# Sixteen residual tiles, and the queries and keys of 32 heads, turned by VectorE from swapped blocks instead of by TensorE

## The chip, the cores and the metric

The kernel runs on one core of one Trainium2 chip, as one program in one launch. The metric is its device time in microseconds (us). The core has a matrix engine (TensorE, PE in the profile), a vector engine (VectorE, DVE), a scalar engine (ScalarE, ACT), a general one (GpSimd, POOL), and the engine that issues the weights' DMAs (SyncE, SP).

## The reference

Two blocks of a model run on the same 256 tokens of width 2048, in float32. The first (`first_block`) is one layer: norm, a projection to the queries, keys and values of 8 + 8 heads and to two gates, two kinds of attention over heads of 128, gated output projections, a feed-forward part of width 5632, and a gated side input. The second (`second_block`) has an even layer (short convolutions, a chunked state space part, attention to 256 memory tokens) and an odd layer (latent attention with 16 heads, and memory attention again). Cut to what the change touches:

```python
# first block: per head of 128
z = q @ k.T * scale                      # causal: stick breaking (sb), or with bias, softmax (ca)
log_keep = where(past, log_sigmoid(-z), 0.0)
between = cumsum(log_keep, reverse=True) - log_keep
a = where(past, exp(log_sigmoid(z) + between), 0.0);  y = a @ v
# residual sums, each of them then normed and multiplied by the next weights
x = x + merged @ w_mix_out
x = x + (silu(g_ff) * u_ff) @ w_ffn_out
x = x + sigmoid(h @ w_ple_gate) * (p @ w_ple_in)
x = x + concatenate([y_a, y_b, y_m]) @ w_out0
# odd layer, latent attention, 16 heads: 128 columns without and 64 with rotation
q_full = concatenate([q_nope, q_rope]);  k_full = concatenate([k_nope, k_rope])
y_c = causal_block_attention(q_full, k_full, v) * silu(z_c)
```

## The kernel before

**The stream.** All weights lie in one stream of 919 units of 512 KB, each 2 chunks of 128 rows by 512 columns. SP loads them one after the other into a ring of four slots, `raw`. For each unit ACT makes the high part `w_hi` (rounded; line 1241), DVE the low part `w_lo` = raw - high (line 1756), and PE runs `unit`: eight matmuls with the high part (line 730: two chunks, two halves of the tokens, high and low part of the activations) and four with the low part (line 736). ACT and DVE work three units ahead (`LEAD`), in a ring of four, so a slot is free when PE has ended the unit before.

**The order.** Everything else is placed beside the stream by hand. A stage is a loop over blocks of 512 output columns and over units; before the split of unit u + 3 (on ACT and DVE) and before unit u (on PE) a hook is called with the unit's number, and what it issues stands there in the engine's queue. All engines run in order. POOL's queue carries the stores and loads of activations. The stages in the trace's order: mem, win (20 blocks of 8 units; the last eight carry the heads), out, mix, ffn, ffo, ple, gate, then ein, dt, ez, sc, eout of the even layer and olow, omem, uq, ukv, zc, oout of the odd one.

**The heads of win.** `attend` handles four heads per iteration of 16 units, four iterations. Head j begins at unit 3j: PE transposes its two halves of q and k (line 808), ACT copies them out of PSUM (`qk_t`, line 1350), PE makes the scores one unit later (lines 815, 816), DVE adds the mask (`z_sb`, line 1867), ACT and DVE make the probabilities, PE transposes them at 3j + 5, DVE copies them (`p_t`, line 1900), and PE makes y at 3j + 6 (line 828). ACT and DVE split y into `y_t_hi` and `y_t_lo` (line 1904). POOL loads q, k and v of a head with two DMAs.

**The residual tiles.** A stage that ends in a sum of the residual stream gives four tiles of 256 x 512. DVE adds (line 1959), POOL stores the tile, and in the following block, at `TURN_AT` = 3, PE transposes it by `turn_tile` (line 767, eight transposes), with ACT and DVE taking the high and low parts straight from PSUM. Already in the kernel before, the eleven `h` tiles of the ffn go another way: POOL stores the tile to `d_h`, loads it back with four DMAs that swap blocks of 32 rows (`h_b`, line 550), and DVE turns within blocks of 32 x 32 (line 1996).

**The latent heads.** `latent_heads` of zc starts a head every second unit: four transposes for q and k (line 1169), and for each second head two for the rotated part (line 1174); a copy by ACT (line 1694), scores one unit later (lines 1184, 1185). DVE also makes the block's gated tile (line 2462) and the heads' output rows (line 2436). Heads of the attention to memory are done by `mem_job`, whose step 0 transposes loaded queries and keys (`m_qkv`, line 916).

## Time and profile before

| | us |
|---|---|
| median of 3 runs (2696.89 to 2697.67) | 2696.9 |
| profiled execution | 2698.77 |
| its span | 2697.2 |
| PE busy | 2679.3 (99%) |
| DVE busy | 1522.2 (56%) |
| ACT busy | 1364.0 (51%) |
| POOL busy | 239.9 (9%) |
| DMA | 597.00 MB, 221 GB/s in the mean |

The profile is one execution; the time of a kernel is the median of runs, so a difference worked out in the trace is taken from the profiled execution and then set against the median. PE is busy nearly all of the span, so what counts in every view is what PE does and what it waits for; the idle time of the others is no cost. L12 stands for line 12 of the kernel, PEld for the loads of weights into PE, which run beside its matmuls.

### The profile page before, as it was taken

How to read it: one execution, taken by the hardware profiler on the slowest of the kernel's cores; microseconds unless marked ns; L12 is line 12 of the kernel's file. 1: busy time of each engine (PE TensorE's matmuls, PEld its weight loads, DVE VectorE, ACT ScalarE, POOL GpSimd, SP SyncE). 2: the span in 40 equal slices, each digit the busy share in tenths (PEclk: the TensorE clock that was granted, in tenths of full speed). 3: DMA queues.
4: the chain of work that ended last, by engine and by line, in shares of the span. 5: the costliest groups of instructions: out<-in, count | busy, mean ns of one | idle time of the engine just before them, and what ended most of it. 6: DMA issues, size and time to landing. Idle time of an engine off the chain costs nothing.

```text
span 2697.2 us, 36246 instructions
## 1 busy us (share of the span) xinstructions
PE 2679.3 (99%) x12375; PEld 2229.3 (83%) x12375; DVE 1522.2 (56%) x1771; ACT 1364.0 (51%) x1822; POOL 239.9 (9%) x344
## 2 busy tenths in 40 slices
PE   9999999999999999999999999999999999999998
PEld 7888888888888888888888888888888889788887
DVE  6444455656555555555454664446777755446754
ACT  6544455654444444444444554446575445555543
POOL 2100011100000000000000001001110000121200
PEclk9999999999999999999999999999999999999999
DMA  8976666666766667676666767667666766675565
GB/s 304 307 227 216 215 230 213 196 233 218 226 208 209 226 208 222 210 225 224 205 207 205 245 216 223 207 209 246 219 223 219 252 207 211 221 267 197 177 215 163
DMA packets 165441, 597.00 MB, mean 221 GB/s; under 512 B 20080, under 2 KB 20128, under 8 KB 164576
## 3 DMA queue, kind: packets, MB, share of 16 engines
q1 hardware_dynamic: 133632, 485.03, 54.9%
q0 software_dynamic: 30992, 109.53, 12.5%
q8 instruction: 66, 1.08, 0.2%
q10 hardware_dynamic: 720, 1.11, 0.1%
q14 instruction: 31, 0.25, 0.0%
HBM read 547.83 MB, written 49.33 MB: 221 GB/s over the span
## 4 chain that ended last, share of the span: by engine, by line
PE 95%; DVE 2%; ACT 1%; issue 1%; DMA 1%; POOL 0%; POOLq 0%; ACTq 0%; SPq 0%; DVEq 0%
PE acc L730 59%; PE acc L736 30%; PE turn L767 1%; DVE w_lo L1756 1%; PE turn L1032 1%; ACT w_hi L1241 0%; PE ps_s L1184 0%; PE ps_s L1185 0%; PE ps_y L828 0%; DMA m_qkv<-d_mem 0%; PE ps_y L937 0%; PE turn L1169 0%; PE ps_s L922 0%; PE ps_s L816 0%; PE turn L1191 0%
## 5 line engine op out<-in xcount | busy, mean ns | idle before, releaser
L1756 DVE TENSOR_TENSOR w_lo<-raw,w_hi 128x1024 fp32r<-128x1024 f32 x919 | 1120.4, 1224 | 940.5 <-ACT w_hi L1241 933.3
L1241 ACT ACTIVATE w_hi<-raw 128x1024 fp32r<-128x1024 f32 x919 | 966.6, 1059 | 926.9 <-PE acc L736 888.9
L730 PE MATMUL acc<-w_hi,x_t_hi 128*128 128x512 f32 (+1 forms) x2400 | 951.5, 396 | 0.0
L730 PE MATMUL acc<-w_hi,x_t_lo 128*128 128x512 f32 (+1 forms) x2400 | 933.0, 389 | 0.0
L736 PE MATMUL acc<-w_lo,x_t_hi 128*128 128x512 f32 (+1 forms) x2400 | 639.9, 388 | 0.0
L736 PEld LDWEIGHTS acc<-w_lo,x_t_hi 128*128 128x128 f32 x2400 | 450.5, 188 | 92.3
L730 PEld LDWEIGHTS acc<-w_hi,x_t_hi 128*128 128x128 f32 x2400 | 450.9, 188 | 90.3 <-issue 1.9
L730 PEld LDWEIGHTS acc<-w_hi,x_t_lo 128*128 128x128 f32 x2400 | 450.9, 188 | 90.1 <-issue 1.9
L730 PE MATMUL acc<-w_hi,ff_t_hi 128*128 128x512 f32 x352 | 137.2, 390 | 0.0
L730 PE MATMUL acc<-w_hi,ff_t_lo 128*128 128x512 f32 x352 | 137.0, 389 | 0.0
L736 PE MATMUL acc<-w_lo,ff_t_hi 128*128 128x512 f32 x352 | 94.1, 389 | 0.0
L730 PE MATMUL acc<-w_hi,z_t_hi 128*128 128x512 f32 x224 | 87.8, 392 | 0.0
L730 PE MATMUL acc<-w_hi,z_t_lo 128*128 128x512 f32 x224 | 87.2, 389 | 0.0
L736 PEld LDWEIGHTS acc<-w_lo,ff_t_hi 128*128 128x128 f32 x352 | 66.1, 188 | 13.8
L730 PEld LDWEIGHTS acc<-w_hi,ff_t_hi 128*128 128x128 f32 x352 | 66.1, 188 | 13.6
L730 PEld LDWEIGHTS acc<-w_hi,ff_t_lo 128*128 128x128 f32 x352 | 66.1, 188 | 13.6
L406 POOL DMA_DIRECT2D d_x<-tile x16 | 11.7, 730 | 559.0 <-DVE tile L1959 352.0
L736 PE MATMUL acc<-w_lo,z_t_hi 128*128 128x512 f32 x224 | 59.9, 389 | 0.0
L730 PE MATMUL acc<-w_hi,o_t_hi 128*128 128x512 f32 x144 | 56.5, 392 | 0.0
L730 PE MATMUL acc<-w_hi,o_t_lo 128*128 128x512 f32 x144 | 56.1, 389 | 0.0
L730 PE MATMUL acc<-w_hi,lat_t_hi 128*128 128x512 f32 x136 | 56.0, 412 | 0.0
L730 PE MATMUL acc<-w_hi,lat_t_lo 128*128 128x512 f32 x136 | 54.0, 397 | 0.0
(394 smaller groups left out, 2601.5 us busy)
## 6 DMA issues: line engine op xcount, KB each, us to landing
raw<-stream SPq DMA_DIRECT2D x919, 512.0 KB, 4.2
d_in<-tile POOLq DMA_DIRECT2D x20, 512.0 KB, 3.7
d_ev<-tile POOLq DMA_DIRECT2D x20, 512.0 KB, 4.4
d_x<-tile POOLq DMA_DIRECT2D x16, 512.0 KB, 4.0
xin<-d_x POOLq DMA_DIRECT2D x16, 512.0 KB, 7.3
qkv<-d_in POOLq DMA_DIRECT2D x32, 192.0 KB, 3.7
d_h<-tile POOLq DMA_DIRECT2D x11, 512.0 KB, 5.9
h_b<-d_h POOLq DMA_DIRECT2D x44, 128.0 KB, 4.2
```

Source lines behind the costliest of these rows:

```text
L406: pool.dma_start(dst[:, :, bass.ds(b.times(NBW), NBW)], tile[slot][:, :, :])\
L730: nc.tensor.matmul(out, src[x][:, chunk + c, t * P:(t + 1) * P], w_hi[:, s, w], start=first and c == 0 and x == 0, stop=False)
L736: mm = nc.tensor.matmul(acc[2 * bank + t][:, 0:width], src[0][:, chunk + c, t * P:(t + 1) * P], w_lo[:, s, w], start=False, stop=last and ...
L767: mm = nc.tensor.transpose(turn[h][:, (c * TH + t) * P:(c * TH + t + 1) * P], src[:, t, at:at + P], ident[:, :])
L1032: nc.tensor.matmul(turn[t][:, w], dec[:, t, h * P:(h + 1) * P], xdt[:, t, w], start=True, stop=True)
L1241: nc.scalar.activation(w_hi[:, u.slot, :], raw[:, u.slot, :], ACT.Copy).then_inc(hi_ready, 1)
L1756: nc.vector.tensor_tensor(w_lo[:, s, :], raw[:, s, :], w_hi[:, s, :].bitcast(F32), ALU.subtract).then_inc(lo_ready, 1)
```

## The change

Three kinds of transposes leave PE, and a step is moved.

Residual tiles: 16 of 20 (`BY_DVE`; out 3 of 4, mix 3, ffo 4, gate 3, eout 3) are written with their columns regrouped, so that each run of 128 stored columns holds one 32-column piece of each of the four 128-column chunks; the later readers read them back through the same view. After the store has landed, POOL loads four blocks (32 partitions x 8 x 128, 128 KB each) into `r_b` (in the out stage through `d_h` into `h_b`), DVE turns them (`turn_blocks`, 128 x 1024) and ACT and DVE make the high and low parts from SBUF. `RES_AT` and `X4_AT` give the units of these steps, the fourth tile of ffo is turned in the gate stage, and out takes units 6 and 7.

Heads of win: the columns of the weights are permuted on the host, q and k of a head are loaded by four DMAs of 32 partitions x 8 x 64 (64 KB) and v by a fifth, and DVE turns q and k two units before the scores (`HEAD_AT_UNIT`: heads at 1, 3, 6, 9). Only the first head's later steps thereby come one unit later than before.

Latent heads: two heads are a pair. Eight block DMAs, one of the rotated part and two of v are loaded per pair, into one buffer for q and one for k, which POOL refills when DVE has turned the pair before; DVE turns a pair with two instructions (`turn_pair`) at every fourth unit. The transposes of the rotated part stay on PE.

The second layer's memory heads (`mem_job(1, ...)`) run one unit later, their last step in the first unit of zc.

```diff
+BY_DVE = {"out": 3, "mix": 3, "ffo": 4, "gate": 3, "eout": 3}
+RES_AT = {"mix": (5, 6, 7), "ffo": (5, 6, 7), "gate": (6, 7, 7)}
+X4_AT = {(2, 1): 0, (2, 6): 1, (3, 5): 2}
+HEAD_AT_UNIT = (1, 3, 6, 9)
+    def natural(a):
+        return a.rearrange("p (c b i) -> p c b i", c=4, i=SQ)
+    def regrouped(a, on=True):
+        return a.rearrange("p (b c i) -> p c b i", b=4, i=SQ) if on else natural(a)
...
         def load_head(j, J, m):
-            for t in range(TH):
-                src = heads[j % 2][:, t, :, bass.ds(m, 1), :].rearrange("p m h d -> p m (h d)")
-                pool.dma_start(qkv[j][:, t, :, :], src).then_inc(at_loaded[j], 16)
+            for b in range(HD // SQ):
+                src = d_in[:, bass.ds(m.times(2 * HD, 3072 * (j % 2) + 2 * SQ * b), 2 * SQ)]
+                pool.dma_start(qk_b[j][b * SQ:(b + 1) * SQ, :, :], src.rearrange("(a j) n -> j a n", j=SQ))\
+                    .then_inc(at_loaded[j], 16)
+            src = d_in[:, bass.ds(m.times(HD, 3072 * (j % 2) + 2048), HD)]
+            pool.dma_start(v_h[j][:, :, :], halves(src)).then_inc(at_loaded[j], 16)
...
+        def load_blocks(dst, src, n):
+            pool.wait_ge(turned, 2 * n)
+            for b in range(P // SQ):
+                pool.dma_start(dst[b * SQ:(b + 1) * SQ, :, :],
+                               src[:, b * P:(b + 1) * P].rearrange("(a j) n -> j a n", j=SQ)).then_inc(blocks_in, 16)
...
-                store_tile(new, At(b), b % 2, s_, v_)
+                store_tile(halves(new), At(b), b % 2, s_, v_)
                 if b < 2:
-                    load_tile(old, At(b + 2), b % 2, [])
+                    load_tile(halves(old), At(b + 2), b % 2, [])
+                if b < BY_DVE[stage]:
+                    pool.wait_ge(tile_moved[b % 2], 16 * (STORED[stage] + b // 2 + 2))
+                    load_blocks(r_b, new[:, b * NBW:(b + 1) * NBW], TURN[turns] + b)
...
-            load_latent(J)
+        for j in range(1, 8):
+            pool.wait_ge(l_qk, j)
+            if j + 1 < 8:
+                load_rope(j + 1)
+            load_q(j)
+            load_k(j)
+            for J in (2 * j, 2 * j + 1):
+                load_v(J)
...
-                if p == 3 * j:
-                    pe.wait_ge(at_loaded[j], At(0, i, 1).times(32, 32))
-                    pe.wait_ge(at_qk, J.times(1, 1))
-                    for x in range(2):
-                        for t in range(TH):
-                            mm = nc.tensor.transpose(turn[0][:, (2 * x + t) * P:(2 * x + t + 1) * P],
-                                                     qkv[j][:, t, x, :], ident[:, :])
-                if p == 3 * j + 1:
+                if p == HEAD_AT_UNIT[j] + 1:
...
-                        if b:
-                            turn_tile(At(turns + b - 1), tile[(b - 1) % 2], *ready(b - 1))
...
-                    mem_job(1, At(4 + j), p - 7 * j - 5)
+                    mem_job(1, At(4 + j), p - 7 * j - 6)
...
-                    nc.scalar.activation(qk_t[s][:, :], turn[0][:, :], ACT.Copy).then_inc(at_qk, 1)
-                    nc.scalar.activation(lqk[s][:, :], turn[0][:, :], ACT.Copy).then_inc(l_qk, 1)
...
+        def turn_blocks(n, count, src, dst):
+            dve.wait_ge(blocks_in, count)
+            dve.wait_ge(turn_lo, 2 * n + 2)
+            nc.vector.transpose(dst[:, :].rearrange("p (c a i) -> p c a i", c=4, i=SQ),
+                                src[:, :, :].rearrange("p a (c i) -> p c a i", c=4)).then_inc(turned, 2)
...
+                if p == HEAD_AT_UNIT[j] - 1:
+                    dve.wait_ge(at_loaded[j], At(0, i, 1).times(80, 80))
+                    dve.wait_ge(at_scores, J.times(1, 1))
+                    nc.vector.transpose(qk_t[s][:, :].rearrange("p (x a i) -> p x a i", x=2, i=SQ),
+                                        qk_b[j][:, :, :].rearrange("p a (x i) -> p x a i", x=2))\
+                        .then_inc(at_qk, 1)
...
-                    last = nc.vector.tensor_tensor(tile[b % 2][:, t, :], acc[2 * (b % 2) + t][:, :],
-                                                   xin[b % 2][:, t, :], ALU.add)
+                    last = nc.vector.tensor_tensor(regrouped(tile[b % 2][:, t, :], b < BY_DVE[stage]),
+                                                   natural(acc[2 * (b % 2) + t][:, :]),
+                                                   regrouped(xin[b % 2][:, t, :], stage == "ffo" and b < BY_DVE["mix"]),
+                                                   ALU.add)
...
+        def turn_pair(j):
+            dve.wait_ge(at_loaded[0], AT_LOADS + 128 * (j + 1))
+            for x, src in enumerate((q_b, k_b)):
+                last = nc.vector.transpose(lqk[:, :, x, :].rearrange("p s (a i) -> p s a i", i=SQ),
+                                           src[:, :, :].rearrange("p a (s i) -> p s a i", s=2))
+            last.then_inc(l_qk, 1)
...
+            if p % 4 == 0 and 0 < p < 32:
+                turn_pair(p // 4)
```

**DVE's order, start of the second block of zc.** `zgt` and `tile_67` are the gated tile, `ybuf` a head's output rows, `lpt` the turned probabilities. Before:

```order
L1756 TENSOR_TENSOR w_lo<-raw,w_hi 128x1024
L2462 SCALAR_TENSOR_TENSOR tile_67<-zgt,tile_67 128x1024
L2436 TENSOR_SCALAR ybuf<-ps_y,lsm 128x128 x2
L2428 RECIPROCAL lsm<-lsm 128x2
L1756 TENSOR_TENSOR w_lo<-raw,w_hi 128x1024
L2431 COPY lpt_184<-turn 128x384
```

Of the changed kernel, the same place, with the blocks of queries `q_b` and keys `k_b`:

```order
L1819 TENSOR_TENSOR w_lo<-raw,w_hi 128x1024
L2593 SCALAR_TENSOR_TENSOR tile_67<-zgt,tile_67 128x1024
L2513 STREAM_TRANSPOSE lqk<-q_b 128x2x256
L2513 STREAM_TRANSPOSE lqk<-k_b 128x2x256
L2567 TENSOR_SCALAR ybuf<-ps_y,lsm 128x128 x2
L2559 RECIPROCAL lsm<-lsm 128x2
L1819 TENSOR_TENSOR w_lo<-raw,w_hi 128x1024
L2562 COPY lpt_190<-turn 128x384
```

The two turns stand behind the gated tile and ahead of the heads' other work.

**DVE's order in win, around the first head's y and the third head's scores** (`sm` and `prob_ca` belong to the head between). Before:

```order
L1904 ISA
L1904 TENSOR_TENSOR y_t_lo<-ps_y,y_t_hi 128x256
L1892 RECIPROCAL sm<-sm 128x2
L1895 TENSOR_SCALAR prob_ca<-prob_ca,sm 128x128
L1895 TENSOR_SCALAR prob_ca<-prob_ca,sm 128x256
L1754 REGISTER_ALU
L1756 TENSOR_TENSOR w_lo<-raw,w_hi 128x1024
L1862 REGISTER_ALU
L1867 SCALAR_TENSOR_TENSOR z_sb<-ps_s,past 128x384
L1754 REGISTER_ALU
L1756 TENSOR_TENSOR w_lo<-raw,w_hi 128x1024
L1899 REGISTER_ALU
```

Of the changed kernel:

```order
L1817 REGISTER_ALU
L1819 TENSOR_TENSOR w_lo<-raw,w_hi 128x1024
L1997 ISA
L1997 TENSOR_TENSOR y_t_lo<-ps_y,y_t_hi 128x256
L1955 REGISTER_ALU
L1960 SCALAR_TENSOR_TENSOR z_sb<-ps_s,past 128x384
L1817 REGISTER_ALU
L1819 TENSOR_TENSOR w_lo<-raw,w_hi 128x1024
L1993 COPY p_t_102<-turn 128x384
```

The first head's `y_t_lo` now stands directly ahead of `z_sb`; before, a split lay between them.

## Rows read from the trace of the kernel before

**Rows 1.** Page, part 1: busy time, share of the span, instructions, by engine.
```profile
PE 2679.3 (99%) x12375; PEld 2229.3 (83%) x12375; DVE 1522.2 (56%) x1771; ACT 1364.0 (51%) x1822; POOL 239.9 (9%) x344
```

**Rows 2.** Page, part 5, the split: group | busy, mean ns | idle before, releaser.
```profile
L1756 DVE TENSOR_TENSOR w_lo<-raw,w_hi 128x1024 fp32r<-128x1024 f32 x919 | 1120.4, 1224 | 940.5 <-ACT w_hi L1241 933.3
L1241 ACT ACTIVATE w_hi<-raw 128x1024 fp32r<-128x1024 f32 x919 | 966.6, 1059 | 926.9 <-PE acc L736 888.9
```

**Rows 3.** Timeline of PE, mix stage: start, us, engine, instruction.
```profile
692.22 1.08 PE L736 MATMUL acc<-w_lo,m_t_hi 128*128 128x512 f32 x4
693.14 1.04 PE L767 MATMUL turn<-ident,tile 128*128 128x128 f32 x8
...
695.86 1.08 PE L736 MATMUL acc<-w_lo,m_t_hi 128*128 128x512 f32 x4
...
698.59 1.07 PE L736 MATMUL acc<-w_lo,m_t_hi 128*128 128x512 f32 x4
```

**Rows 4.** Groups of PE, the transposes of a residual tile (columns as in rows 2).
```profile
L767 PE MATMUL turn<-ident,tile 128*128 128x128 f32 x160 | 20.7, 272 | 0.0
```

**Rows 5.** Groups of DVE, by form.
```profile
L1996 DVE STREAM_TRANSPOSE h_t<-h_b 128x1024 f32<-128x1024 f32 x11 | 13.7, 1242 | 6.2 <-DMA h_b<-d_h 6.2
...
L1959 DVE TENSOR_TENSOR tile<-acc,xin 128x512 f32<-128x512 f32 x16 | 10.3, 686 | 2.7 <-PE acc L736 2.7
```

**Rows 6.** Timeline of POOL, one tile of the ffn stage.
```profile
799.59 0.75 POOL L546 DMA_DIRECT2D d_h<-tile  x1 [32.93 <-DVE tile L1981]
803.79 2.34 POOL L550 DMA_DIRECT2D h_b<-d_h  x4 [3.45 <-DMA d_h<-tile]
```

**Rows 7.** Timeline of PE, win stage, two heads; brackets: idle before, releaser.
```profile
526.94 1.07 PE L736 MATMUL acc<-w_lo,x_t_hi 128*128 128x512 f32 x4
...
530.14 1.07 PE L736 MATMUL acc<-w_lo,x_t_hi 128*128 128x512 f32 x4
531.50 0.49 PE L815 MATMUL ps_s<-qk_t 128*128 128x128 f32 x2 [0.30 <-ACT qk_t L1350]
```

**Rows 8.** Timeline, win stage, second head of an iteration: DVE and PE.
```profile
382.02 0.56 DVE L1867 SCALAR_TENSOR_TENSOR z_sb<-ps_s,past 128x384 f32<-128x384 f32 x1 [0.60 <-PE ps_s L816]
...
386.51 1.23 DVE L1756 TENSOR_TENSOR w_lo<-raw,w_hi 128x1024 fp32r<-128x1024 f32 x1 [3.93 <-ACT w_hi L1241]
...
387.65 0.55 DVE L1900 COPY p_t<-turn 128x384 f32<-128x384 f32 x1
...
388.26 0.70 PE L828 MATMUL ps_y<-p_t,qkv 128*128 128x256 f32 x2 [0.45 <-DVE p_t L1900]
```

**Rows 9.** Timeline, zc stage, start of its second block.
```profile
2474.49 0.38 PE L1169 MATMUL turn<-ident,lq 128*128 128x128 f32 x2
...
2474.93 0.38 PE L1174 MATMUL turn<-ident,lrope 128*128 128x128 f32 x2
...
2476.79 1.23 DVE L2462 SCALAR_TENSOR_TENSOR tile<-zgt,tile 128x1024 f32<-128x1024 f32 x1 [1.08 <-ACT zgt L1726]
...
2477.93 0.60 DVE L2436 TENSOR_SCALAR ybuf<-ps_y,lsm 128x128 f32<-128x128 f32 x2
...
2478.23 0.39 PE L1184 MATMUL ps_s<-lqk 128*128 128x128 f32 x2
```

**Rows 10.** Timeline of PE in the uq stage.
```profile
2346.21 1.07 PE L736 MATMUL acc<-w_lo,lat_t_hi 128*128 128x512 f32 x4
2349.45 0.77 PE L916 MATMUL turn<-ident,m_qkv 128*128 128x128 f32 x4 [2.17 <-DMA m_qkv<-d_mem]
...
2353.37 0.85 PE L736 MATMUL acc<-w_lo,lat_t_hi 128*128 128x512 f32 x3
```

**Rows 11.** Windows: us, each engine's busy time, granted clock, DMA share, GB/s.
```profile
2349.80:2353.20 3.40, 3.40 (x11) 2.72 (x10) 0.00 (x0) 2.91 (x4) 0.00 (x0) 0.51 1.00 393
```

**Rows 12.** Page, part 6: DMAs, count, KB each, us from issue to landing.
```profile
raw<-stream SPq DMA_DIRECT2D x919, 512.0 KB, 4.2
...
h_b<-d_h POOLq DMA_DIRECT2D x44, 128.0 KB, 4.2
```

More of the change, by code:

```diff
@@ L280, in program @@
     act_moved = sem("act_moved")
+    blocks_in = sem("blocks_in")
+    OUT_MOVES, RES_MOVES = 16 + 4 * 16, 4 * 16
+    BLOCKS = {"out": 0, "mix": 0, "ffo": 3, "gate": 7, "eout": 10}
     turned = sem("turned")
@@ L696, in _ @@
             store_block(kv_v, "ukv", b, 0, At(b), b % 2)
+            if b == 0:
+                for s in range(2):
+                    pool.wait_ge(tile_moved[s], 16 * (STORED["ukv"] + 1))
+                load_rope(0)
+                load_q(0)
             if b == 2:
@@ L866, in residual @@
                 for k in range(units):
-                    if k == TURN_AT:
-                        if b:
-                            turn_tile(At(turns + b - 1), tile[(b - 1) % 2], *ready(b - 1))
-                        elif before:
-                            before()
+                    if before and (b, k) == (0, TURN_AT):
+                        before()
                     source(src_turns, k)
                     unit(At(U0[stage] + b * units + k), src, UCH * k, b % 2, k == 0, k == units - 1)
-            return lambda: turn_tile(At(turns + 3), tile[1], *ready(3))
-        def from_sums(stage):
-            return lambda b: (sums_out, B0[stage] + b + 3)
-        before = residual("mix", m_t, 8, TURN["mix"], TURN["ffn"], from_sums("mix"),
+            if BY_DVE[stage] == 4:
+                return None
+            return lambda: turn_tile(At(turns + 3), tile[1], *ready)
+        before = residual("mix", m_t, 8, TURN["mix"], TURN["ffn"], (sums_out, B0["mix"] + 3 + 3),
                           lambda: turn_tile(At(TURN["mix"] + 3), tile[0], tile_ready, 6))
@@ L893, in _ @@
             ffn_pair(1, i, None)
-        before = residual("ffo", ff_t, 22, TURN["ffo"], TURN["ple"], from_sums("ffo"), None)
+        before = residual("ffo", ff_t, 22, TURN["ffo"], TURN["ple"], (sums_out, B0["ffo"] + 3 + 3), None)
         pe.wait_ge(ple_lo, 1)
@@ L900, in _ @@
             unit(At(U0["ple"] + b), ple_t, 0, b % 2, True, True)
[L901 removed]
+        before = residual("gate", x_t, 8, TURN["ple"], TURN["x3"], (tile_ready, 4 + 3 + 3), before)
         def mem_job(n, J, p):
@@ L1265, in high, with high_blocks @@
                 last.then_inc(turn_hi, 1)
+        def high_blocks(n, src, dst, b, g=None):
+            act.wait_ge(turned, 2 * (n + 1))
+            if g is None:
+                at = dst[0][:, 4 * b:4 * b + 4, :].rearrange("p c t -> p (c t)")
+                last = nc.scalar.activation(at, src[:, :], ACT.Copy)
+            else:
+                for c in range(4):
+                    last = nc.scalar.activation(dst[0][:, 4 * b + c, :], src[:, c * TOK:(c + 1) * TOK], ACT.Copy,
+                                                scale=gain[:, g + 4 * b + c:g + 4 * b + c + 1])
+            last.then_inc(turn_hi, 2)
         def square(src, col, b, count):
@@ L1406, in beside @@
                         tile_out(b - 1)
+                    if b and k == RES_AT[stage][1]:
+                        high_blocks(turns + b - 1, r_t, dst, b - 1, g)
                     if not b:
@@ L1917, in _, with beside_out @@
         for n in range(4):
+            def beside_out(p):
+                if n and p == 6:
+                    turn_blocks(TURN["mix"] + n - 1, OUT_MOVES * n, h_b, h_t)
+                if n and p == 7:
+                    low_blocks(TURN["mix"] + n - 1, h_t, m_t, n - 1)
             for b in range(2):
-                splits("out", 4, 8 * n + 4 * b, 0, 0,
-                       lambda k: low(At(TURN["mix"] + n - 1), m_t, At(n - 1)) if n and (b, k) == (0, 2) else None)
+                splits("out", 4, 8 * n + 4 * b, 0, 0, lambda k: beside_out(4 * b + k))
                 if b == 0:
@@ L1929, in _ @@
             dve.wait_ge(turned, 2 * (TURN["mix"] + n))
-            nc.vector.tensor_tensor(tile[0][:, :, :], part[:, 0, :, :], part[:, 1, :, :], ALU.add)\
-                .then_inc(tile_ready, 1)
+            for t in range(TH):
+                last = nc.vector.tensor_tensor(regrouped(tile[0][:, t, :], n < BY_DVE["out"]),
+                                               natural(part[:, 0, t, :]), natural(part[:, 1, t, :]), ALU.add)
+            last.then_inc(tile_ready, 1)
         dve.wait_ge(act_once, 3)
@@ L1942, in beside @@
                 def beside(k):
-                    if b and k == TURN_AT:
-                        low(At(turns + b - 1), dst, At(b - 1), g)
+                    if b and k == RES_AT[stage][0]:
+                        turn_blocks(turns + b - 1, moved_blocks(stage, b - 1), r_b, r_t)
+                    if b and k == RES_AT[stage][2]:
+                        low_blocks(turns + b - 1, r_t, dst, b - 1, g)
                     if not b:
```

294 lines of the change are left out of this document (176 added, 118 removed).

## The prediction

> **What bounds the kernel now.** I read the busy line first. PE is busy 2679.3 us of a span of 2697.2 [rows 1]; DVE, which gets much of the moved work, is at 56% and ACT at 51%. The costliest groups show why [rows 2]. The split of the weights costs ACT 1.06 us and DVE 1.22 us for each of 919 units, and both spend much of their time waiting: ACT 888.9 us for PE's last matmul on the ring slot, DVE 933.3 us for ACT. So the chain goes PE, ACT, DVE, and PE is never short of weights in a plain stretch. The timeline of PE then gives the prices [rows 3]: two plain units start 2.73 us apart (695.86 to 698.59), which is twelve matmuls at 0.227. Every transpose on PE therefore lies on the path that sets the end, and what leaves PE is gained, unless something new makes PE wait. What leaves ACT or DVE is worth nothing in itself.
>
> How much later may DVE be? ACT may start on a slot when unit u-1 has ended, so the low part for unit u+3 is ready 1.06 + 1.22 = 2.3 us into unit u [rows 2]; PE reads it after two more units and eight matmuls of the third, at 3 x 2.72 + 8 x 0.227 = 10.0. DVE has about 7.7 us to give away at a place, if ACT keeps up. That is the cover for nearly all that the change lays on DVE.
>
> **Part 1, residual tiles: sixteen tiles, eight transposes each.** In the timeline the unit with the transposes of a tile in front of it takes 695.86 - 692.22 = 3.64 us against 2.73 for the next one [rows 3], so 0.91 a tile; I take 0.90. The group of all of them has 160 transposes, 20 tiles [rows 4]; 128 go. 16 x 0.90 = **14.4 us off**. What comes in their place: one DVE transpose of 128x1024, which the kernel already does for the ffn's inputs in 1.24 us [rows 5], a low part of about 1.22 us as before, adds with a rearranged output (0.69 us each [rows 5]; a strided result could make them slower, I take the same), and on POOL four block DMAs, issued in 2.34 us, after the store has landed [rows 6]. On DVE this is some 1.3 us a tile, against 7.7 us of slack: nothing. Bounds: if a DVE addition with a broken-up pattern took twice as long, two of them are 1.4 us more, still covered: PE's next block writes the other two banks and doesn't wait for these adds. So the term stays between 14.4 and 14.6 as long as the blocks come in time, which is rival D.
>
> **Part 2, the sixteen heads in the win stage.** The four PE transposes of q and k cost 530.14 - 526.94 = 3.20 against 2.72, so 0.48 us [rows 7], in each of 16 heads. 16 x 0.48 = 7.7 us. In one of the four heads of an iteration PE also waits for ACT's copy of q and k: its matmuls end 0.91 after 530.14, at 531.05, and the scores start at 531.50 [rows 7]. That 0.45 goes too, since DVE turns q and k two units before the scores: 4 x 0.45 = 1.8. The other stall of an iteration doesn't go. PE waits 0.45 in front of the second head's y matmul, at 388.26, for DVE's copy of the turned probabilities, at 387.65 [rows 8]. This copy stands behind a w_lo at 386.51, which waits for ACT, which is held up by abs, exp, a table load and ln on z_sb; and z_sb was made at 382.02. The order of the changed program puts head 0's y_t_lo (with its wait for ACT's y_t_hi) straight ahead of this z_sb in the same hook, where before it ran a unit earlier. y_t_lo works on 128x256, where the p_t copy of 128x384 takes 0.55 [rows 8], so I put it at 0.4 us (an estimate); z_sb is that much later, and the whole chain with it: 4 x 0.4 = 1.6 lost. Together 7.7 + 1.8 - 1.6 = 7.9, taken as **8 us off**. Bounds: 7.7 + 1.8 + 1.8 = 11.3 if the stall vanished entirely, 5.9 if the delay were twice the 0.45 that PE waits now. DVE's own transposes of 128x512 are not in the trace; half of 1.24 is 0.62, at most 1.24. They stand in hooks where DVE otherwise waits for ACT. POOL now issues five DMAs a head instead of two, 2.34 for four [rows 6] and one more like the store's 0.75, so 12.4 us for four heads in an iteration of sixteen units, over 43 us: nothing.
>
> **Part 3, the sixteen latent heads.** Four transposes again, 2474.93 - 2474.49 = 0.44 us [rows 9], so 16 x 0.44 = 7.0 us. Against this stands a new wait. The two turns of a pair stand first in the hooks at every fourth unit. At three of them (the starts of blocks 2, 3 and 4 of the stage) DVE comes late: it first has the gated tile, 2476.79 with 1.23 us, and ends at 2478.02 or a little before, since the next instruction starts at 2477.93 [rows 9]. Then come two transposes of 128x512 together, about 0.62 each: the operands are ready at 2479.2. PE wants to start the scores at 2478.23 in the trace, and 0.4 sooner without its four transposes: 2477.8. That is 1.4 us of idle PE three times, 4.2 us. The first pair of the stage has the loads in front of it: ten issues after the last store of keys; it may cost 0 to 2 us, I take 0. Net 7.0 - 4.2 = **2.8 us off**. Bounds: 7.0, and 0.8 with the 2 us; beyond that only by rival C.
>
> **Part 4, the memory head moved one unit later.** PE waits 2.17 us at 2349.45 for the DMA of its keys [rows 10]; the matmuls behind it run at half the clock: the granted clock is 0.51, the lower of the two levels, for 3.4 us [rows 11], after that pause. From 2346.21 to 2353.37 the unit takes 7.16 us. With the step one unit later, PE comes to it at 2346.21 + 0.91 + 2.72 = 2349.84, and the keys had landed by 2349.45. Then the unit costs 3.20: **4.0 us off**. The margin is 0.4 us. Bounds: 4.0, and 1.9 (2.17 of pause less a little, with the half clock staying). The last step moves to the first unit of the next stage with all that it holds on each engine, the same instructions as before, so nothing.
>
> **The sum.** 14.4 + 8 + 2.8 + 4.0 = 29.2 us. The profiled execution took 2698.8, so 2669.6; the median of the runs shown is 1.9 below the profiled one, 2696.9, so about 2668. With 1 us for the first pair and 1 us for the heads' bounds the forecast's own range is 2664 to 2671.
>
> **Rivals.**
> A, *no new stalls*. DVE's queue at the three boundaries is not as late as I read it (its waits end with ACT's, and ACT has two copies fewer per pair), or the heads' stall goes. For: ACT no longer copies q and k out of PSUM in either stage, and stands in these chains. Against: the row of the gated tile is released by ACT's gate work [rows 9], which stays. Gain 14.4 + 11.3 + 7.0 + 4.0 = 36.7, so 2660; with half of the difference 2664. Chance 12%.
>
> B, *the new pauses drop the clock*. In the trace a pause of 2.17 us was followed by 3.4 us at 0.51 [rows 10, 11]: half of these 3.4 us, 1.7, was lost. If 1.4 us does that too, three times 1.7 is 5 us: 2673. Against: pauses of 0.3 and 0.45 [rows 7, 8] cost no such thing, the units around them are at full speed. Chance 13%.
>
> C, *the 256-byte runs load slowly*. Heads' and pairs' blocks are 64 columns wide, so each run is 256 bytes; h_b has 512-byte runs and lands in 4.2 us with four in flight beside the weights' 4.2 [rows 6, 12]. If the half-size runs go at half speed, landing is 8 us, and each pair has only about that between the release of its buffer and its turn: 0.7 us for six pairs and 4 us for the first is 8 us more, 2676. Heads have 43 us and don't notice. Chance 12%. The Trainium skill, "DMA: Bandwidth & Descriptors", in the table at its top, speaks for this one: it states 512 bytes as the smallest transfer that goes at line rate, below which the engine reads, modifies and writes. The trace shows only 512-byte runs for blocks, so no row here decides it.
>
> D, *slower than before: the blocks of the residual tiles come late and DVE's wait for them starves PE*. Now DVE waits for a DMA that depends on POOL, the store and four more DMAs. Its place is the hook at unit 5 or 6 of the block after. From the end of a block: two adds 1.4, a store whose landing lets the blocks issue 4.2 after it was issued (799.59 to 803.79), 2.3 for issuing, 4.2 for landing, and about 1 for another issue in the queue: 13.1 [rows 6, 12]. DVE gets there at about 13.2 (it has just finished the low part of unit 7, counted from 0, which is ready 2.3 into unit 4: 4 x 2.72 + 2.3). So it waits little, and has 7.7 less 1.3 to give: PE waits only from a landing 19.6 us after the block's end. To be slower than before by 5.4 us it would need (29.2 + 5.4) / 16 = 2.2 us at each tile, so landings at 21.8, 8.7 us beyond what the rows give. They have 3.45 of waiting for a store's landing [rows 6]; the wait would have to be over three times that. Then 2702 or more. Chance 5%, of which 2% stops within 0.2%.
>
> **How the numbers follow.** Forecast 58% (2664 to 2671), A 12%, B 13%, C 12%, D 5%. What a measurement of this kernel can tell from no change is about 0.2%, 5.4 us. All of the first four are faster by more: 95%. Same 2%, slower 3%. The range 2660 to 2677 holds the forecast, most of A, B and C.
>
> **What would show it.** In the changed profile: the transposing units of mix, ffo, gate and eout back at 2.72; L767's count 32; no idle at PE's first score of an iteration, and 0.8 to 0.9 idle at the y matmul that now has 0.45; PE idle 1.4 us for l_qk at three places of the zc stage and none elsewhere there; the memory head's transposes at full clock without a wait for m_qkv. If PE's waits for w_lo after a block DMA come up in the mix or eout stage, part 1 is wrong. If the time is over 2677, landings are the reason, or DVE's adds.

## The result, and the profile after

The changed kernel takes 2683.4 us (median of 5 runs, 2681.5 to 2685.8) against 2696.9 (5 runs, 2695.0 to 2697.7): the ratio is 0.995, 95% interval 0.9939 to 0.9962. It is faster by 13.5 us where 29 were forecast, and outside the range given (2660 to 2677). The profiled execution took 2681.5, 17.3 less than that of the kernel before; its span is 2679.9.

The page of the changed kernel, part 1 and from part 5 the two groups of the split (columns as in rows 2):

```profile
PE 2651.9 (99%) x12119; PEld 2202.8 (82%) x12119; DVE 1552.4 (58%) x1824; ACT 1349.4 (50%) x1787; POOL 330.5 (12%) x507
...
L1819 DVE TENSOR_TENSOR w_lo<-raw,w_hi 128x1024 fp32r<-128x1024 f32 x919 | 1117.5, 1223 | 880.2 <-ACT w_hi L1278 874.0
L1278 ACT ACTIVATE w_hi<-raw 128x1024 fp32r<-128x1024 f32 x919 | 964.8, 1060 | 894.3 <-PE acc L801 807.4
```

256 transposes left PE, and its busy time fell by 27.4 us [rows 1]; the span fell by 17.3 only. So about 10 us came back as idle PE (the busy times of both kernels hold a stretch at the lower clock, so this is no clean count of work). ACT's wait for PE shrank from 888.9 to 807.4 [rows 2] without ACT having more to do: it now waits for something else. The waits by reason say for what (engine, line, what it waited for: us in total, times, longest):

```profile
ACT w_hi L1278 <- DMA raw<-stream: 78.0, 51, 5.7
...
DVE r_t L1855 <- DMA r_b<-d_x: 29.8, 10, 5.4
...
POOL h_b L551 <- DMA d_h<-tile: 22.5, 3, 10.3
...
DVE h_t L1855 <- DMA h_b<-d_h: 17.0, 3, 6.5
```

In the kernel before, ACT's wait for the weights was 29.0 us, 23 times. DVE waits 46.8 us for blocks, which it never did in these stages.

The time from one unit's last matmul to the next one's, summed by stage, from the two traces (stages that differ by less than 0.2 us left out):

| stage | before | after | difference | forecast |
|---|---|---|---|---|
| win (heads) | 475.5 | 466.9 | -8.5 | -8 |
| out | 89.8 | 91.7 | +1.9 | -2.7 |
| mix | 91.2 | 88.5 | -2.7 | -2.7 |
| ffn | 479.6 | 480.5 | +0.9 | 0 |
| ffo | 242.1 | 239.4 | -2.8 | -2.7 |
| gate | 90.7 | 90.5 | -0.2 | -3.6 |
| ein | 230.7 | 233.4 | +2.8 | 0 |
| eout | 159.6 | 156.9 | -2.7 | -2.7 |
| uq and ukv | 108.5 | 104.3 | -4.2 | -4.0 |
| zc (latent heads) | 134.8 | 133.0 | -1.7 | -2.8 |

(The fourth tile of ffo is turned in gate, so by the stage in which PE saved them the 16 x 0.9 are 2.7 in out, mix, ffo and eout and 3.6 in gate.) The heads, the memory head and, in this execution, ten of the sixteen tiles do what was forecast; the latent heads give 1.1 us less. Nearly all of the rest of the miss is in out, gate and ein, with 0.9 us in ffn.

This profiled execution was the fastest of the changed kernel's five. The experiments below leave mix and ffn alone in seven kernels, and there the two stages together took 568.8 to 573.2 us, against 568.9 in the changed kernel and 570.8 before: in six of the seven the three tiles of mix gained 0.3 us at most or lost up to 2.4, with a forecast of 2.7 gained. PE's late units stand at the start of mix's block 3 and of ffn. So the table flatters mix.

**The out stage.** Timeline of the changed kernel around the second tile:

```profile
614.62 1.44 POOL L536 DMA_DIRECT2D gates<-d_in  x2 [12.31 <-DVE tile L2029]
...
616.05 0.72 POOL L558 DMA_DIRECT2D d_h<-tile  x1
...
622.13 1.06 ACT L1278 ACTIVATE w_hi<-raw 128x1024 fp32r<-128x1024 f32 x1 [5.65 <-DMA raw<-stream]
...
627.02 2.34 POOL L551 DMA_DIRECT2D h_b<-d_h  x4 [10.25 <-DMA d_h<-tile]
...
633.75 1.25 DVE L1855 STREAM_TRANSPOSE h_t<-h_b 128x1024 f32<-128x1024 f32 x1 [6.50 <-DMA h_b<-d_h]
```

Two gate loads of 512 KB stand ahead of the store of the tile in POOL's queue. The store lands 11 us after its issue, where rows 6 have 4.2, and DVE waits 6.5 us for the blocks behind it. By the prediction's slack PE would have lost next to nothing by that, but the weights were late already: ACT had itself waited 5.65 us for them at 622.13, after DVE's wait for the first tile's blocks. And of the landing, 11 us is against one quick case; in the kernel before, the median of eleven such stores was 5.9 us:

```profile
d_h<-tile POOLq DMA_DIRECT2D x11, 512.0 KB, 5.9
```

PE then waits for DVE's low part:

```profile
636.16 1.93 PE L801 MATMUL acc<-w_lo,y_t_hi 128*128 128x512 f32 x4 [2.71 <-DVE w_lo L1819]
```

And the windows of these microseconds (columns as in rows 11):

```profile
628.00:632.00 4.00, 4.00 (x20) 3.30 (x19) 0.00 (x0) 0.13 (x1) 1.35 (x3) 1.00 0.94 259
632.00:636.00 4.00, 1.45 (x7) 0.87 (x5) 2.25 (x2) 0.91 (x1) 0.00 (x0) 1.00 0.06 12
636.00:640.00 4.00, 3.84 (x10) 3.05 (x11) 3.82 (x6) 4.00 (x5) 0.00 (x0) 0.57 0.43 142
```

DMA is at 0.94 before DVE gets its blocks, and at 0.06 after: the weights stop, because `load` on SP reloads a slot of `raw` only when DVE has made the low part from it. And PE's pause of 2.71 us is followed by a granted clock of 0.57 over 4 us. With both this tile costs 4.6 us.

**The gate stage.** There the turn and the parts stand at units 6 and 7, right ahead of a chain at the block's end: sigmoid on ACT, product, sum and scaling on DVE, squares on ACT, and only then the next high part. Timeline of the changed kernel at the end of block 1:

```profile
1516.50 1.25 DVE L1855 STREAM_TRANSPOSE r_t<-r_b 128x1024 f32<-128x1024 f32 x1 [1.54 <-DMA r_b<-d_x]
...
1517.79 1.72 ACT L1312 ACTIVATE x_t_hi<-r_t,gain 128x256 fp32r<-128x256 f32 x4 [0.61 <-DVE r_t L1855]
1519.41 1.05 ACT L1278 ACTIVATE w_hi<-raw 128x1024 fp32r<-128x1024 f32 x1
1519.54 1.68 DVE L1868 SCALAR_TENSOR_TENSOR x_t_lo<-r_t,gain,x_t_hi 128x256 fp32r<-128x256 f32 x4 [0.68 <-ACT x_t_hi L1312]
1520.36 1.24 ACT L1514 ACTIVATE pl_sig<-acc,rstd 128x512 f32<-128x512 f32 x2
...
1524.85 0.64 ACT L1321 ACTIVATE junk<-x_raw 128x512 f32<-128x512 f32 x1 [3.24 <-DVE x_raw L2134]
...
1526.09 2.94 ACT L1278 ACTIVATE w_hi<-raw 128x1024 fp32r<-128x1024 f32 x3
```

`pl_sig` has no idle time in front of it: ACT came to it late, 2.4 us after PE had ended the block (at 1517.94). In the kernel before it waited 1.60 us there for PE and started as soon as the block had ended:

```profile
1531.13 1.27 ACT L1461 ACTIVATE pl_sig<-acc,rstd 128x512 f32<-128x512 f32 x2 [1.60 <-PE acc L736]
```

From the start of `pl_sig` to the next high part it is 5.73 us instead of 5.07 (1536.20 in the kernel before), since DVE makes its low part within the chain: ACT waits 3.24 us for `x_raw`, not 2.55. The next high part starts at 1526.09, and PE, which has used up the three units prepared for it, waits:

```profile
1527.19 0.50 PE L795 MATMUL acc<-w_hi,x_t_hi 128*128 128x512 f32 x1 [1.02 <-ACT w_hi L1278]
```

The same stands at the end of block 2 (1.76 us idle, at 1551.00), and in unit 3 of ein (0.80 for the tile and 1.44 for the high part).

**Heads and latent heads.** The stall at the second head's y grew from 0.45 [rows 8] to 0.77 of idle matmul time, by the y_t_lo that stands ahead of z_sb: z_sb starts 0.38 us after the scores have ended, where it was 0.04, and from its start to that of the copy of the probabilities it is 5.63 us in both kernels. The first of three latent boundaries shows the wait that the prediction had at 1.4:

```profile
379.94 0.42 DVE L1997 TENSOR_TENSOR y_t_lo<-ps_y,y_t_hi 128x256 f32 x1 [0.41 <-ACT y_t_hi L1415]
380.28 0.55 DVE L1960 SCALAR_TENSOR_TENSOR z_sb<-ps_s,past 128x384 f32<-128x384 f32 x1
...
386.52 0.70 PE L886 MATMUL ps_y<-p_t,v_h 128*128 128x256 f32 x2 [0.77 <-DVE p_t L1993]
```

```profile
2460.82 0.70 DVE L2513 STREAM_TRANSPOSE lqk<-q_b 128x512 f32<-128x512 f32 x1
2461.44 0.67 DVE L2513 STREAM_TRANSPOSE lqk<-k_b 128x512 f32<-128x512 f32 x1
...
2462.17 0.49 PE L1221 MATMUL ps_s<-lqk 128*128 128x128 f32 x2 [1.35 <-DVE lqk L2513]
```

In the uq stage the memory head's transposes start at 2338.49 with no wait, in a unit of 3.20 us (2337.58 to 2340.78), against 7.16 [rows 10]. The DMA rows of the page (columns as in rows 12) and of the DMA view give the landings:

```profile
r_b<-d_x POOLq DMA_DIRECT2D x52, 128.0 KB, 5.7
...
qk_b<-d_in POOLq DMA_DIRECT2D x64, 64.0 KB, 3.4
...
q_b<-d_q POOLq DMA_DIRECT2D x32, 64.0 KB, 3.8
```

The blocks of 256-byte runs land sooner than the ones of 512-byte runs; they are also half the size.

### The profile page after: what moved, and what is told of

It reads as the page before. It is cut to its first block, busy times and chain, and to the rows that moved or that the text cites. A ratio compares the mean times of both kernels' runs of the same rounds, so it can differ in the third digit from the quotient of the medians.

```text
span 2679.9 us, 35985 instructions
## 1 busy us (share of the span) xinstructions
PE 2651.9 (99%) x12119; PEld 2202.8 (82%) x12119; DVE 1552.4 (58%) x1824; ACT 1349.4 (50%) x1787; POOL 330.5 (12%) x507
## 3 DMA queue, kind: packets, MB, share of 16 engines
q0 software_dynamic: 36032, 119.50, 14.6%
## 4 chain that ended last, share of the span: by engine, by line
PE 89%; DMA 3%; DVE 3%; issue 3%; ACT 1%; POOL 1%; POOLq 0%; ACTq 0%; SPq 0%; DVEq 0%
PE acc L795 56%; PE acc L801 28%; DMA r_b<-d_x 1%; DMA d_x<-tile 1%; DMA d_h<-tile 1%; DVE w_lo L1819 1%; PE turn L1084 1%; ACT w_hi L1278 1%; POOL r_b L551 0%; PE ps_s L1221 0%; PE ps_s L1222 0%; DMA h_b<-d_h 0%; PE ps_y L886 0%; PE ps_y L989 0%; PE ps_s L873 0%
## 5 line engine op out<-in xcount | busy, mean ns | idle before, releaser
L1278 ACT ACTIVATE w_hi<-raw 128x1024 fp32r<-128x1024 f32 x919 | 964.8, 1060 | 894.3 <-PE acc L801 807.4
L795 PEld LDWEIGHTS acc<-w_hi,x_t_lo 128*128 128x128 f32 x2400 | 450.9, 188 | 90.5 <-issue 1.9
L581 POOL DMA_DIRECT2D d_h<-tile x11 | 8.0, 727 | 381.6 <-DVE tile L2092 381.6
```

The costliest lines, as they stand in the source:

```text
L581: pool.dma_start(halves(d_h), tile[0][:, :, :]).then_inc(cols_in, 16)
L795: nc.tensor.matmul(out, src[x][:, chunk + c, t * P:(t + 1) * P], w_hi[:, s, w], start=first and c == 0 and x == 0, stop=False)
L1278: nc.scalar.activation(w_hi[:, u.slot, :], raw[:, u.slot, :], ACT.Copy).then_inc(hi_ready, 1)
```

## The experiments

Times by stage are formed as in the table above. All kernels are edits of the changed kernel. The ratios are to the runs of the kernel before beside each of them, whose medians were 2697.0 to 2698.2 us; the changed kernel's own 2683.4 stands beside a 2696.9, so differences to it carry about 1 us of shift. Each kernel was traced in one execution.

**e1, the store ahead of the gate loads (out stage).**

```diff
-            if n < 2:
-                load_gates(n, (n + 2) * NBW, n + 3)
             pool.wait_ge(tile_ready, n + 3)
 ...
             load_blocks(h_b, d_h, TURN["mix"] + n)
+            if n < 2:
+                load_gates(n, (n + 2) * NBW, n + 3)
```

> Only the order of POOL's queue in the out stage is changed: the store of a tile and its four block loads go ahead of the two gate loads (1 MB) of the block pair after next. Theory 1 (the gate loads ahead of the store in the same queue make it land after 10 us instead of 4, and DVE's wait of 6.5 us for the second tile's blocks then starves PE): the store lands in 4 to 6 us, the stall of 4.6 us in the out stage goes, the stage is 87.1 us instead of 91.7, the median about 2679. Rival (it is the amount of traffic beside the weights, whatever the order): the stage stays within 1 us of 91.7 and the median at 2682 to 2684.

Measured: 2679.8 us, ratio 0.9928 (0.9915 to 0.9942). The out stage is 87.04 us. POOL's wait for the store, in the timeline of e1 at the same tile:

```profile
610.35 0.73 POOL L556 DMA_DIRECT2D d_h<-tile  x1 [13.49 <-DVE tile L2029]
614.18 2.33 POOL L551 DMA_DIRECT2D h_b<-d_h  x4 [3.10 <-DMA d_h<-tile]
```

3.8 us from the store's issue to that of the blocks instead of 11, and DVE does not wait for the blocks of this stage at all, instead of 17.0 us. The same bytes move; their order was the cause, as shown. In this execution ffn is 484.3, 3.8 us longer than the changed kernel's: there DVE waits 6.12 us for mix's third tile and PE idles 2.06. Whether the edit has a part in that, no run shows; e8, which has the edit too, has no such wait, but its mix is another one.

**e2, the old tile's load behind the blocks (mix, ffo, gate, eout).** In `residual` of POOL, `load_tile(halves(old), At(b + 2), ...)` is moved behind `load_blocks`.

> In the residual stages the load of the old residual tile (512 KB) is issued behind the four block loads instead of ahead of them. Theory 1 (order in the queue): in the gate stage the blocks land 2 us sooner, DVE's wait of 1.5 us for them goes, the stalls of 1.3 and 2.1 us in gate shrink by at least 1 us each: median about 2681. Theory 2 (the stalls of the gate stage come from the high and low parts standing in the last hook of a block, right ahead of the chain of sigmoid, product, sum and squares that frees ACT for the next unit): the gate stage stays at 90.4 us and the stall of 2.7 us at the start of ein stays too.

Measured: 2679.4 us, ratio 0.9928 (0.9915 to 0.9942). Gate 90.33 and ein 235.3: theory 2. The stalls of 1.4 and 1.9 us in gate are still there, and that of ein is 4.6. The median is lower by 4 us than that of the changed kernel's own runs, but none of the four stages edited got shorter by more than 0.12 us in the trace; behind them, ffn is 0.9 us shorter and ein 1.9 longer. The 4 us stay unexplained, and I take nothing from them.

**e3, the third head one unit later.** `HEAD_AT_UNIT = (1, 3, 7, 9)`.

> One number: the third head of an iteration starts at unit 7 instead of 6, so that its masked scores on DVE stand behind the copy of the second head's turned probabilities, which they held up. Theory: the wait of PE in front of the second head's y goes, 1.03 us in each of four iterations, the win stage is 462.8 us instead of 466.9, the median about 2679. Rival (the y matmul there waits for something else that takes its place, the split of the weights behind ACT's long chain): the stall moves to another unit of the iteration and the stage stays at 466 to 467.

Measured: 2678.8 us, ratio 0.9931 (0.9917 to 0.9944); win 462.75 us. The timeline of e3 shows the order turned round:

```profile
380.47 0.56 DVE L1993 COPY p_t<-turn 128x384 f32<-128x384 f32 x1 [0.39 <-PE turn L879]
381.13 0.56 DVE L1960 SCALAR_TENSOR_TENSOR z_sb<-ps_s,past 128x384 f32<-128x384 f32 x1
...
383.67 0.59 PE L886 MATMUL ps_y<-p_t,v_h 128*128 128x256 f32 x2
```

The y matmul has no idle time in front of it. Two other units of the iteration got longer, by 0.64 and 0.68 us, by the work of the third head that now stands in them, and the units it left are shorter by as much; what remains is the stall, 1.03 us in each iteration.

**e4, the pairs turned at the end of the unit before.** `turn_pair((p + 1) // 4)` stands behind `rotate((p + 1) // 4)` at p % 4 == 3, and no longer first at p % 4 == 0.

> The turns of a pair of latent heads stand at the end of the hook of unit 4j-1 instead of first in that of unit 4j, so ahead of the gated tile at a block's start. Theory (DVE comes late to them behind the gated tile): the three stalls of 1.65 us go, the zc stage is 128.1 us instead of 133.0, the median about 2678.5. Rival (the loads of the 256-byte runs are only just in time): DVE then waits for the blocks of q and k at the earlier place, PE's stalls stay or come at seven places instead of three, and the stage is 133 us or more.

Measured: 2677.5 us, ratio 0.9923 (0.9909 to 0.9937); zc 129.1 us. All three boundary stalls are gone. One of 0.97 us is left at the first pair whose loads POOL issues in this stage, the one that the prediction put at 0 to 2 us: DVE waits for it once, 3.5 us:

```profile
DVE lqk L2513 <- DMA k_b<-d_kv: 3.5, 1, 3.5
```

**e5, gate's tiles back to PE.** `BY_DVE["gate"] = 0`, with `turn_tile` and the parts from PSUM at unit 3 as in the kernel before. The kernel leaves out the matching of column orders in the even layer's sum, so three tiles of unlike order are added there; no time depends on it.

> The gate stage's three tiles go back to PE's transposes (and are stored with their columns in the old order); everything else as in the changed kernel. Theory (three tiles there win 2.7 us of transposes and lose more in waits): the gate and ein stages together go from 323.9 us back to the 321.4 of the kernel before, the median falls by 2 to 3 us against the changed kernel's 2683.4. Rival (the waits there come from the stages ahead, mix and ffo, that load by blocks): gate and ein stay above 323.

Measured: 2683.1 us, ratio 0.995 (0.9936 to 0.9964). Gate 89.8 and ein 230.7, 320.5 together against 323.9: as the theory has it, 3.4 us shorter. The median did not follow (a fall of 2 to 3 us was expected). In the traced execution out, mix and zc were 4.4 us longer than the changed kernel's, 1.8 of them in zc, where DVE waits 2.4 us for the first pair loaded in that stage; the other executions have no trace. So in the changed kernel DVE's three tiles of gate cost more than PE's: the two stages together are 320.5 us here, and 323.6 to 324.6 in the changed kernel and its four edits that leave them alone.

**e6, gate's tiles one block later.** Turn, high and low part at units 3, 4, 5 of the block after next; the third tile in ein at 1, 2, 3.

> The gate stage's tiles are turned by DVE one block later, at its units 3 to 5 (the third tile in the first block of ein, units 1 to 3), when their blocks have long landed, instead of in the last two units of the next block. Theory (DVE's wait for the blocks holds up the low parts, and with them the reload of weights, which waits for the low part; and the work in the last hook delays the chain at the block's end): the stalls of 1.3, 2.1 and 2.7 us go, gate and ein together are 318 us instead of 323.9, the median 2677. Rival (the traffic of store, old tile and blocks itself makes the weights late, wherever the turn stands): at least 3 of the 6 us stay.

Measured: 2686.1 us, ratio 0.9964 (0.9952 to 0.9976), 2.7 us above the changed kernel's median where a fall to 2677 was expected. Gate has no stall (87.04 us, better than expected), but unit 3 of ein is 10.1 us longer than without a stall (13.75 us against 3.61): PE's transposes of the fourth tile wait there for the third tile's low part, which now comes behind the chain at the stage's end. Half right: the place was the cause, and the new place of the third tile was a worse one.

**e7, ffo's turn early.** `RES_AT["ffo"] = (2, 3, 4)`.

> In the ffo stage, where three tiles were turned at unit 5 without any stall of PE, the turn stands at unit 2 (high part 3, low part 4). DVE comes to it 5.0 us after the block's end, and the blocks land at 13 to 16. Theory 1, the slack as the prediction had it (7.7 us less 1.3 of work): PE loses 13 to 16 - 5.0 - 6.4, so 2 to 5 us per tile, and nothing else. Theory 2 (SP reloads a slot only when DVE has made its low part, so a wait of DVE stops the weights as well): the DMA engines run nearly empty while DVE waits, then carry a burst, ACT waits for raw weights after it, and PE loses about as much again: 5 to 9 us per tile, 15 to 27 us for the stage, and the median 2698 to 2710.

Measured: 2689.7 us, ratio 0.9969 (0.9957 to 0.9981); ffo 248.0 us, 8.6 more, 2.9 a tile. Theory 1 in size. Theory 2's mechanism is seen, its size is not: DVE waits 9.97 us at the first tile (blocks landed at 1298.8, 15.1 us after the block's end), and in the windows of e7 the DMA is empty right after, when no slot has been given back:

```profile
1290.00:1293.00 3.00, 3.00 (x15) 2.49 (x14) 0.00 (x0) 1.54 (x5) 0.00 (x0) 1.00 0.91 313
1293.00:1296.00 3.00, 3.00 (x15) 2.49 (x14) 0.00 (x0) 0.00 (x0) 1.65 (x3) 1.00 0.26 87
1296.00:1299.00 3.00, 3.00 (x14) 2.25 (x12) 0.17 (x1) 0.00 (x0) 0.70 (x2) 1.00 0.40 131
1299.00:1302.00 3.00, 0.90 (x4) 0.67 (x4) 2.18 (x2) 1.90 (x5) 0.00 (x0) 1.00 0.00 0
```

This tile cost PE 3.1 us by the lengths of its two late units. A wait of 10 us for 3.1: a slack of about 7 us was real there. The next tile is 22 units away in this stage, so the ring fills up again before it.

**e8, e1 + e3 + e4, and the tiles of gate and mix one block later, as gate's in e6.**

> The changed kernel with the third head at unit 7, the out stage's store and blocks ahead of the gate loads, the pairs of latent heads turned at the end of unit 4j-1, and the tiles of mix and gate turned one block later. If the stalls have the causes that these edits take away and are independent: win 462.8, out 87.0, mix 88.4, ffn 479.6, gate 88.0, ein 230.7, zc 129.1 and all else as before it: 18 us less than the changed kernel's profiled 2681.5, so 2664, and the median 2663 to 2667. If taking one stall away uncovers another in the same place, 2667 to 2674.

Measured: 2672.3 us, ratio 0.9907 (0.9891 to 0.9922). Every stage came out as listed or up to 1 us better but ein (241.4) and ffn (481.2), where the third tile's low part holds up PE's transposes of the fourth (by 1.43 us of idle PE in ffn), in the timeline of e8 for ein:

```profile
1568.02 1.66 DVE L1887 SCALAR_TENSOR_TENSOR x_t_lo<-r_t,gain,x_t_hi 128x256 fp32r<-128x256 f32 x4
...
1569.83 1.51 PE L838 MATMUL turn<-ident,tile 128*128 128x128 f32 x6 [7.75 <-DVE x_t_lo L1887]
```

**e9, the third tile in the gaps.** As e8, with the two tiles at units 2, 4, 5 and the third as here (the two calls at the end are ACT's, between `pl_sig` and the squares, and DVE's, in the first hook of ein; ffn has the like in its hooks 0 and 1):

```diff
+def tile_at(stage, b, k, step):
+    late = stage in ("mix", "gate")
+    if late and (b, k, step) == (3, 7, 0):
+        return 2
+    at = (2, 4, 5) if late else RES_AT[stage]
+    return b - 1 - late if b > late and k == at[step] else None
 ...
+            if b == 3:
+                high_blocks(TURN["x3"] + 2, r_t, x3_t, 2, 64)
 ...
+            if k == 0:
+                low_blocks(TURN["x3"] + 2, r_t, x3_t, 2, 64)
```

> As the combined kernel before it, but the tiles of mix and gate are turned at unit 2 of the block after next (high part 4, low part 5), and the third tile, which the next stage needs, at unit 7 of block 3; its high part stands in ACT's idle time between sigmoid and squares (gate) or in the next stage's first hook (mix), its low part in the next stage's first or second hook. Theory (PE's transposes of the fourth tile at unit 3 of ein waited 7.8 us for the third tile's low part, which stood too late behind the chain at the block's end): the stall of 10.6 us in ein and of 1.6 us in ffn go to under 1 us each, all else as in the combined kernel: about 11 us less, the profiled execution 2662 to 2664, the median 2660 to 2663. Rival (DVE's wait for the third tile's blocks at unit 7 holds up the gate chain instead): a stall of 1 to 4 us at unit 3 of ein and a median of 2664 to 2667.

Measured: **2660.2 us**, ratio to before 0.9864 (0.9847 to 0.988), the fastest of all and 23 us under the changed kernel. Gate 87.0, ein 230.7, ffn 479.6. From its page:

```profile
span 2657.5 us, 35985 instructions
...
PE 2644.7 (100%) x12119; PEld 2201.1 (83%) x12119; DVE 1553.5 (58%) x1824; ACT 1347.9 (51%) x1787; POOL 328.3 (12%) x507
```

The instructions are those of the changed kernel, one for one in number. No unit of out, mix, ffn, ffo, gate and ein is over 0.15 us longer than the same unit where it is shortest in the traces of the changed kernel and its edits. Of the 22.4 us between this span and the changed kernel's, 1.9 are in the first stage, which no edit touches (see the end of the next section).

**e10, only gate's high and low parts moved.** The changed kernel with the parts at units 2 and 3 of the following block (third tile as in e9); DVE's turn stays at unit 6.

> Against the changed kernel only the high and low parts of the gate stage's first two tiles are moved, from the last unit of a block to units 2 and 3 of the block after (the third tile's to ACT's and DVE's idle time around the end of the stage). DVE's wait for the blocks and the turn stay at unit 6. If the work right ahead of the gate chain makes the stalls: the gate stage goes from 90.4 to 87.0 us and ein from 233.4 to 230.7, the median falls by 5 to 6 us against the changed kernel's 2683.4, so 2677 to 2678. If it is DVE's wait for the blocks and the late weights: at least half of the 6 us stays, the median is 2680 to 2683.

Measured: 2676.0 us, ratio 0.992 (0.9907 to 0.9934). Gate 87.04, ein 230.72: all of the 6.1 us. The wait for the blocks and the late weights are still there, in e10's timeline:

```profile
1519.30 1.25 DVE L1864 STREAM_TRANSPOSE r_t<-r_b 128x1024 f32<-128x1024 f32 x1 [1.11 <-DMA r_b<-d_x]
1519.43 2.11 ACT L1284 ACTIVATE w_hi<-raw 128x1024 fp32r<-128x1024 f32 x2 [2.50 <-DMA raw<-stream]
```

They cost nothing in that stage. What cost was 1.7 us of work on ACT and on DVE at the one place without slack; the edit moves both pieces, so it does not tell ACT's share from DVE's (in the timeline above, 2.4 us of lateness are ACT's and 0.7 DVE's). The profiled execution is only 2.9 us shorter than the changed kernel's, since out, mix and ffn, which the edit leaves alone, were 5.0 us longer in it (and the first stage 1.9 shorter).

## Why the prediction was wrong

The direction and 13.5 of 29 us came; the failed step is one, in part 1: "On DVE this is some 1.3 us a tile, against 7.7 us of slack: nothing", and "the term stays between 14.4 and 14.6 as long as the blocks come in time". What the stages gave, against 14.4: 14.4 - 4.6 (out) - 0.9 (ffn) - 3.4 (gate) - 2.7 (ein) = 2.8 us. Three things were wrong with it.

- **The slack was worked out for a plain stretch and used at a block's end.** In a plain stretch 7.7 us is about right (e7: 10 us of waiting cost 3). It holds only while the units ahead are ready: in out, a wait of 6.50 us idled PE for 2.71, so 3.8 us of slack were left there, behind ACT's own wait of 5.65 for weights. But in gate the slack is used up by the kernel's own chain, 1.24 us on ACT, 1.22 and 1.29 on DVE, 1.24 on ACT behind PE's last matmul, and only then the next high part. The prediction never read the timeline there, and named only DVE's transposes and low part, not that ACT's high part (1.7 us, no longer at unit 3 but at unit 7) stands in the same queue ahead of the sigmoid. 6.1 us, shown by e10 for ACT's and DVE's parts together.
- **The landing of a store was taken from a place where nothing stood ahead of it.** Rival D's sum used 4.2 us from [rows 6], one tile of the ffn. That tile was a quick one: the median of the eleven such stores before was 5.9 us. In out, POOL of the changed kernel issues 1 MB of gate loads ahead of the store, and the prediction allowed "about 1 for another issue in the queue". It was 11 us instead of 4.2. The second tile's blocks landed at 633.7, 26.6 after PE had ended its block (607.1), beyond the point of 19.6 that rival D gave for PE's first loss; 4.5 of these us are handed on from the first tile, for whose blocks DVE had waited 5.5 us without a loss of PE, so that the second tile's sum came at 613.0 (from the block's end to POOL's next issue behind the sum it is 7.5 us, and 3.0 in e1). 4.6 us, shown by e1. The rival was right as a mechanism at one tile of sixteen, wrong as one for all.
- **A wait of DVE also stops the weights**, since SP's reload waits for the low part; the traffic then comes in bursts and the next store and blocks land later (mix: blocks 8 us after issue, DVE 5.2 us late at the third tile). That lateness handed on in this way also makes the 0.9 us in ffn is how I read the trace; no experiment isolates it, but e2, which issues mix's blocks sooner, and e9, which moves mix's turns, both have ffn at 479.6. It is not small in other executions: up to 5.1 us in mix and ffn together (573.2 against 568.1 in e9).

The other terms, by their own steps. **Heads:** -8.5 for -8. 0.48 a head was right; the stall at the second head's y is longer by 0.3 us in each iteration, for 0.4 forecast. The trace has the delay of z_sb by 0.34 as stated, and e3, which takes z_sb out of the way, takes away the whole stall. **Latent heads:** -1.7 for -2.8. Three stalls of 1.35 us of idle cost 1.65 each by the unit's length, 4.9 instead of 4.2; the other units of zc are 6.6 us shorter, not 7.0; DVE's turns take 0.70 and 0.67, not 0.62. Place and reason were right (e4). **Memory head:** -4.2 for -4.0.

Rivals. A, no new stalls: not so in the changed kernel, but its 2660 is what e9 reaches. B, the pauses drop the clock: at the three pauses of 1.35 us the granted clock stayed 1.00 (window 2462.20 to 2465.20), so not there; it did drop in out, behind 2.71 us. C, slow 256-byte runs: `q_b` and `qk_b` land in 3.8 and 3.4 us, and e4 turns seven pairs one unit earlier with one wait of 3.5 us. The only waits for such blocks are at the first pair that POOL loads in zc: 0.2 us in the changed kernel, up to 2.4 in the kernels that turn it at the same unit (e5), so the prediction's "0 to 2 us" for it was a fair range. The Trainium skill's page "DMA: Bandwidth & Descriptors" states, in the table at its top, at least 512 bytes for line rate. No run here isolates that: the blocks of 256-byte runs are also half the size, and this pair's loads are ten issues in a row. D: above.

Something stays open: the changed kernel's runs spread over 4.3 us, e9's over 2.3. The out stage of the kernels that leave it alone was 91.7, 91.4, 91.4, 93.4, 93.3, 89.2, 91.4 and 93.3 us, so where DVE waits for a DMA the time seems to be the DMA's and to vary; each of these is one execution of another kernel, and no kernel was traced twice. The first stage, which no edit touches, took 94.7 to 94.9 us in five of the twelve traces and 96.3 to 97.2 in the other seven, the changed kernel's among these; why is not known. I take both as the reason why the medians of single edits do not add up, while the stages they touch do.

## What to carry to other kernels

Slack is a property of a place, not of a kernel: before moving work under a busy engine's shadow, read the timeline at the very unit it goes to, and count every engine's piece of it, above all ahead of a chain that crosses engines. Where a DMA's landing becomes a wait, list what its queue issues just ahead of it; here an issue cost 0.7 us, but the 1 MB of two loads put off the landing behind them by 7 us (e1). And an in-order engine that frees the buffers of a stream throttles the stream whenever it waits (DMA share 0.06 in out, 0.00 in e7).

## What the runs showed of the hardware

Where the clock falls was not to be read from the length of a pause alone. After idle times of 1.35 us (zc) and 1.76 us (gate) of the changed kernel, and 2.10 us in e7 (with another 0.46 right behind), the granted clock stayed at 1.00; after 2.71 us in out it was 0.52, the lower level, over 3.2 us. But in e7 two shorter pauses, 1.22 and 0.48 us, stood ahead of a window at 0.56:

```profile
1363.32 1.20 PE L801 MATMUL acc<-w_lo,ff_t_hi 128*128 128x512 f32 x4 [1.22 <-DVE w_lo L1819]
1364.99 0.47 PE L795 MATMUL acc<-w_hi,ff_t_hi 128*128 128x512 f32 x1 [0.48 <-ACT w_hi L1278]
```

DVE's additions with a regrouped output took 686 ns for 128x512, to the nanosecond what rows 5 have without it. Its transposes are dearer per element when small: 1.245 us for 128x1024, 0.67 to 0.71 for 128x512.
